# One kernel for two transformer blocks: filter network and short convolution moved inside the first projection, and each norm and operand split moved to the head of the phase that uses it

## The reference

```python
z = rmsnorm(h, mix_norm[j]) @ mix_w_in[j]            # layer 0 of the first block, 3328 columns
y_a = rwkv7_bidir(z[..., :RWKV_COLS], ...)           # 1792 columns
y_b = hyena_bidir(z[..., RWKV_COLS:], ...)           # 1536 columns
h = h + jnp.concatenate([y_a, y_b], axis=-1) @ mix_w_out[j]

def hyena_bidir(z, short_w, short_b, ...):
    u = dwconv_centred(z, short_w, short_b)          # 3 taps along the tokens
    x0, x1, v = u[..., :C], u[..., C:2 * C], u[..., 2 * C:]
    h = hyena_filters(L, ...)                        # 3 sine layers of 64, then 64 -> 2 x 512,
                                                     # times a decay, over the root of its squares' sum
    s = (v * x1)
    y = irfft(rfft(s, 2L) * rfft(kern(h), 2L))[:L] + s * bias
    return y * x0
```

## Time and profile before

| | |
|---|---|
| time, median of 3 runs | 3489.85 us (3485.0 to 3491.21) |
| time of the profiled execution | 3489.5 us |
| its span | 3487.7 us |
| PE busy | 3120.9 us (89%) |
| DVE, ACT, POOL busy | 1628.6, 1314.7, 89.5 us |
| mean granted TensorE clock | 0.925 of full speed |

### The profile page before, as it was taken

How to read it: one execution, slowest core, us unless ns; L and a number is a source line. 1 busy time by engine, 2 the same in 40 slices (tenths; PEclk the granted TensorE clock), 3 DMA queues, 4 the chain that set the end, 5 groups by cost and what they waited for, 6 DMA issues and landing times. The chain is left out here.

```text
span 3487.7 us, 47358 instructions
## 1 busy us (share of the span) xinstructions
PE 3120.9 (89%) x19958; PEld 2433.7 (70%) x19958; DVE 1628.6 (47%) x2294; ACT 1314.7 (38%) x2020; POOL 89.5 (3%) x190
## 2 busy tenths in 40 slices
PE   7948688779999889889999878889999898889999
PEld 5824477767777667667777666567888775568887
DVE  2152555545445346745454336654333348543333
ACT  3210434324333333544333333654424235545151
POOL 0000000001000000000000010000000010100000
PEclk9959777789999999999999989999999899989999
DMA  3110100026444222225444222002323130013222
GB/s 126 63 40 24 41 3 2 3 74 190 162 146 141 89 85 85 76 83 178 164 142 149 76 70 81 1 12 74 100 94 101 52 123 3 1 61 97 97 97 85
DMA packets 223521, 286.67 MB, mean 82 GB/s; under 512 B 7555, under 2 KB 163459, under 8 KB 217172
## 3 DMA queue, kind: packets, MB, share of 16 engines
q1 hardware_dynamic: 214580, 229.73, 20.8%
q0 software_dynamic: 7680, 51.91, 4.3%
q10 hardware_dynamic: 1056, 2.10, 0.2%
HBM read 281.62 MB, written 2.10 MB: 81 GB/s over the span
## 5 line engine op out<-in xcount | busy, mean ns | idle before, releaser
L231 DVE TENSOR_TENSOR weights_low_all<-weights,weights_high_all 128x2048 fp32r<-128x2048 f32 x196 | 449.9, 2295 | 672.1 <-ACT weights_high_all L225 668.4
L225 ACT CAST weights_high_all<-weights 128x2048 fp32r<-128x2048 f32 x196 | 373.5, 1906 | 646.6 <-PE ps L239 636.3
L237 PE MATMUL ps<-ffn_h_high,weights_high_all 128*128 128x512 f32 x704 | 277.8, 395 | 0.9 <-DVE weights_low_all L231 0.9
L239 PE MATMUL ps<-ffn_h_high,weights_low_all 128*128 128x512 f32 x704 | 274.4, 390 | 0.0
L238 PE MATMUL ps<-ffn_h_low,weights_high_all 128*128 128x512 f32 x704 | 274.4, 390 | 0.0
L237 PE MATMUL ps<-mlp_h_high,weights_high_all 128*128 128x512 f32 x512 | 201.0, 393 | 3.1 <-DVE weights_low_all L231 1.8
L239 PE MATMUL ps<-mlp_h_high,weights_low_all 128*128 128x512 f32 x512 | 199.5, 390 | 0.0
L238 PE MATMUL ps<-mlp_h_low,weights_high_all 128*128 128x512 f32 x512 | 199.5, 390 | 0.0
L237 PE MATMUL ps<-weights_high_all,mlp_hid_high 128*128 128x512 f32 x512 | 199.2, 389 | 0.0
L238 PE MATMUL ps<-weights_low_all,mlp_hid_high 128*128 128x512 f32 x512 | 199.2, 389 | 0.0
L239 PE MATMUL ps<-weights_high_all,mlp_hid_low 128*128 128x512 f32 x512 | 199.2, 389 | 0.0
(11 more groups left out here) (548 smaller groups left out, 6373.2 us busy)
## 6 DMA issues: line engine op xcount, KB each, us to landing
mod_w<-in_w_mod POOLq DMA_DIRECT2D x48, 1024.0 KB, 5.2
weights<-in_ffn_w_up SPq DMA_DIRECT2D x88, 512.0 KB, 5.0
weights<-in_w_mlp_in SPq DMA_DIRECT2D x32, 1024.0 KB, 5.5
weights<-in_w_mlp_out SPq DMA_DIRECT2D x32, 1024.0 KB, 5.0
weights<-in_ffn_w_down SPq DMA_DIRECT2D x24, 768.0 KB, 4.4
weights<-in_mix_w_in SPq DMA_DIRECT2D x13, 1024.0 KB, 5.1
weights<-in_na_w_qkv SPq DMA_DIRECT2D x12, 1024.0 KB, 5.2
weights<-in_w_in SPq DMA_DIRECT2D x12, 1024.0 KB, 5.8
```

Of the source, the lines that this page charges most:

```text
L225: nc.scalar.copy(st.high[s][:], st.raw[s][:]).then_inc(st.high_done, 1)
L231: nc.vector.tensor_tensor(st.low[s][:], st.raw[s][:], st.high[s][:], ALU.subtract).then_inc(st.split_done, 1)
L237: nc.tensor.matmul(out, lh, rh, start=start, stop=False)
L239: return nc.tensor.matmul(out, ll, rh, start=False, stop=stop)
```

## The change

What it does, in five parts. First, `MixIn` (on the `Up` class of the feed-forward layers) projects all 13 groups in one phase, unrolled, with the norm at its head; between groups PE does one piece of the filter network, the transposes or the column sums; the first six groups' sums go from PSUM straight through the three taps, and the filter's squares, sums and differences are on POOL. Second, the transform has tables and scratch of its own for the way back, and goes back by frequency tile outermost. Third, `add_product_phase` splits its operand itself and takes tile by tile in its first group; the reload of x is issued by ACT. Fourth, `ple_phase` and `project_heads_phase` begin with `Norm`, whose last four tiles are transposed between the products of the first four. Fifth, the loads of the first two `mix_w_out` groups are no longer held back.

```diff
 def add_product_phase(...):
-                        for t in range(TT):
-                            if q == 0:
-                                pe.wait_ge(added, half * TT + (t + 1))
+                        if half == 0 and q == 0:
                             for k in range(n):
...
+                                pe.wait_ge(tile_low, k + 1)
+                                for t in range(TT):
+                                    mm = product(half, q, t, k, a, False)
...
             @block.scalar
...
+                for k in range(KT):
+                    nc.scalar.copy(split[0][:, k, :], src[:, k, :]).then_inc(tile_high, 1)
                 for g in range(2 * NQ):
...
+                    if x_from is not None and g == 0:
+                        act.wait_ge(tile_low, KT)
+                        act.dma_start(cx.x[:], x_from.rearrange("(t p) c -> p t c", p=P)).then_inc(x_back, 16)
...
+class MixIn(Up):
...
+    FILTER_IN, FILTER_OUT, SQUARES, TURNS = (0, 2, 4), (6, 7), (8, 10), {8: (0, 1, 2), 9: (3,)}
...
+    def pool(self, pool, d, turned):
...
+        for t in range(TT):
+            a, b = (self.taken[:, 2 * (t % 2) + q, :] for q in range(2))
+            pool.wait_ge(self.decayed, 2 * t + 2)
+            if t >= 2:
+                pool.wait_ge(self.sq_sum, t - 1)
+            for q, side in enumerate((a, b)):
+                nc.gpsimd.tensor_tensor(self.square(t, q), side, side, ALU.mult).then_inc(self.squared, 1)
...
+            nc.gpsimd.tensor_tensor(y.h_sum[:, t, :], a, b, ALU.add).then_inc(self.joined, 1)
+            nc.gpsimd.tensor_tensor(y.h_dif[:, t, :], a, b, ALU.subtract).then_inc(self.joined, 1)
...
+    def tensor(self, pe, norm):
+        self.behind(pe, norm)
+        self.beside_tensor(pe, 0)
+        for g in range(1, self.n):
+            self.group(pe, g, lambda j: self.free(pe, g - 2, j) if g >= 2 else None)
+            self.beside_tensor(pe, g)
...
+    def vector(self, dve):
...
+            if g - 1 in self.FILTER_OUT:
...
+                        dve.wait_ge(self.out_sum, n + 1)
+                        if t >= 2:
+                            dve.wait_ge(self.joined, 2 * (t - 1))
+                        nc.vector.tensor_tensor(self.taken[:, 2 * (t % 2) + q, :], ps[:, 4 + n % 4, :], self.decay[:, t, :],
+                                                ALU.mult).then_inc(self.decayed, 1)
...
 def hyena_phase(...):
-                    pe.wait_ge(joined, 2 * TT)
-                    pe.wait_ge(inverse, 32)
...
+                for f in range(TT):
+                    pe.wait_ge(joined, 2 * (f + 1))
+                    for k in range(TT):
                         for q in range(2):
...
 def project_heads_phase(...):
+                norm.begin(pe)
+                G.wait(pe, 0)
+                for k in range(4):
+                    norm.ready(pe, k)
+                    for t in range(TT):
+                        mm = latent(0, t, k) if n_latent else value(0, 0, t, k)
+                    norm.turn(pe, k + 4)
+                mm.then_inc(st.used_up, 1)
+                norm.ready(pe, KT - 1)
...
 def ple_phase(...):
+                            for k in range(4):
+                                norm.ready(pe, k)
...
+                                norm.turn(pe, k + 4)
+                            mm.then_inc(st.used_up, 1)
+                            norm.ready(pe, KT - 1)
+                            turn_p()
```

More of the change, by code:

```diff
@@ L561, in wait_channel_sum @@
         eng.wait_ge(G.st.used_up, g + (G.g0 + 1))
[L564 to L588, removed]
-                    for j in range(2):
-                        wait_channel_sum(act, G, g, j, summed)
-                        nc.scalar.copy(z[:, bass.ds(g * 2 + j, 1), :],
-                                       cx.ps[:, 2 * par + j:2 * par + j + 1, :]).then_inc(copied, 1)
-                each_group(act, G, "high", group)
-            @block.vector
-            def _(dve):
-                each_group(dve, G, "low", lambda g, par: None)
 def token_groups(w, splits):
@@ L1130, in _, with ple_phase @@
                 down.vector(dve)
-def ple_phase(nc, cx, tag, split, p_in):
+def ple_phase(nc, cx, tag, norm, split, p_in):
     st = cx.stream
@@ L1195, in _ @@
             def _(act):
-                for k in range(2):
-                    act.wait_ge(turned, k + 1)
-                    nc.scalar.copy(pT[0][:, k, :], cx.ps[:, 4 + k, :]).then_inc(pT_high, 1)
+                norm.scalar(act)
                 def group(g, par):
@@ new lines, in mix_in_phase, with _ @@
+def mix_in_phase(nc, cx, norm, mix, d):
+    st = cx.stream
+    with nc.Block() as block:
+        @block.sync
+        def _(sp):
+            st.load(sp, st.used + 2)
+        @block.gpsimd
+        def _(pool):
+            mix.pool(pool, d, norm.turned)
+        @block.tensor
+        def _(pe):
+            mix.tensor(pe, norm)
+        @block.scalar
+        def _(act):
+            norm.scalar(act)
+            mix.scalar(act)
+        @block.vector
+        def _(dve):
+            norm.vector(dve)
+            mix.vector(dve)
@@ L1282, in hyena_phase @@
+def hyena_phase(nc, cx, d, y):
     ps = cx.ps
@@ L3335, in ple @@
                 h = parts(hx, f"ple_h{l}")
-                norm_phase(nc, cx, f"pn{l}", gain(f"ple_norm{l}"), split=h)
-                ple_phase(nc, cx, f"ple{l}", h, d["p"][l, 0])
+                xn = hx.enter_context(nc.sbuf_tensor(f"ple_xn{l}", [P, TT, D], F32))
+                norm = Norm(nc, cx, hx, f"pn{l}", gain(f"ple_norm{l}"), h, [xn[:, t, :] for t in range(TT)])
+                ple_phase(nc, cx, f"ple{l}", norm, h, d["p"][l, 0])
         if first <= 0 < last:
```

552 lines of the change are left out of this document (292 added, 260 removed).

## The result

The changed kernel takes 3376.29 us (median of 4 runs, 3375.04 to 3377.17) against 3489.7 before: the ratio is 0.9677, 95% interval 0.966 to 0.9694, so 113 us or 3.2% faster. The forecast was 3366, with 3350 to 3392 around it. The profiled execution took 3376.68 us with a span of 3374.8; its mean granted clock is 0.945 (before 0.925), and PE is busy 92% of the span.

What follows compares the result with a forecast made beforehand. PE was busy 89% of the span, so time was to be had only where it idled or ran slowly; 82.5 + 4.2 + 19.5 − 3.2 + 11.2 + 9.2 = 123.4 off 3489.5 gave 3366.1 us, range 3350 to 3392.

Steps and rivals of the forecast that it cites:

- The mixer: First mixer, from first product to hyena's last DVE operation: 279.1 us against 361.66, a gain of 82.5 us.
- To the transform: First mixer, between projection and transform: copy out of PSUM, square root with its table load, reciprocal and barrier, 2.8 us.
- The work between groups: First mixer: filter network's products 9.4, column sums 6.9 and transposes 1.8 us at full clock between projection groups, together 18.1.
- Thirteen groups: First mixer: the projection's 13 groups of products take 144.0 us; the 16 transposes among them are a separate 1.8.
- Output projections: At no and twice ao, PE starts 5.0 us earlier plus a clock credit, 19.5 us together; mo gains 4.2.
- The 1.5 for the clock: At no and both ao: first group 1.5 us faster each, as PE idles 2 us instead of 7.
- mo's wait for x: In mo, group 1 waits for the reloaded x and a remainder behind it; between 0 and 1.4 us lost.
- Norms at the head: Norms moved into nn, pn and an, with PE idle about 5.1 us before group 1: −3.2, 11.2 and 9.2 us.
- two credits of 8 us at the lower end: Range's lower end, 3350: 8 us if short stalls keep the clock, another 8 if transposes fall where PE waits anyway.
- Rival A: First mixer's projection: PE waits for POOL's chain or DVE's list, up to three stalls, 3384 to 3390 us; chance 0.13.
- B: Rival: the mixer gains as forecast but the other nine sites give nothing, 3407 us; chance 0.07.
- C: Rival: frequent short stalls hold PE at the lower clock for the whole first projection, costing 125 us, 3491; chance 0.03.

Runs made afterwards that it cites:

- e2: Changed kernel with the 32 column sums spread, one behind each three products of groups 9 and 11, instead of two pieces of sixteen; 3372.4 us (0.9667).
- f1: Changed kernel with part four undone, the five norms of ple and the head projections again in phases of their own; 3389.2 us (0.9722).
- f2: Changed kernel with part three undone, operands of mo, no and both ao split in their own phase, SP reloading x; 3401.2 us (0.9749).
- g1: The changed kernel itself, unedited, measured and profiled a second time; 3381.0 us (0.9698).
- g3: Changed kernel with each of POOL's squares, sums and differences done three times; 3389.0 us (0.9719).
- g4: Changed kernel with each of POOL's operations done five times; 3423.2 us (0.9815).

## Why the prediction was right, and where it was off

- **The mixer.** "To the transform" and what follows took 87.6 us as forecast (87.8), and the first product came 0.6 us early. The work between groups took 19.4 us for 18.1: the layers and outputs 10.25 for 9.4, the sums 7.5 for 6.9, the transposes 1.7. The term that was mis-sized is "Thirteen groups", 144.0, with 1.8 for the transposes among them: together they took 152.1 us, 6.3 more. The sum held that work between groups runs at full clock in the company of products; most of it did, but the products behind the two pieces of sums did not. e2 shows 4.8 us of the 6.3. By the starts in the timeline the rest is some 0.4 us more at the lower rate at the head and 0.1 at each of about 14 changes between the kinds of products; no run shows it by itself. No run undoes the mixer's part of the change either: its 75.8 us are read from the traces, and agree with what f1 and f2 leave of the 113 (75 to 85). Nor is there a run for the earlier loads of `mix_w_out` alone.
- **Output projections.** The 5.0 us at each were there (4.85, from 7.0 to 2.1 us of idle time). The 1.5 for the clock was right at one of the three sites in the first profile and at none in g1: the prediction took 2 us of idling as too short for the clock to fall, and it fell 24 times of 30. That the table has 15.6 for the 13.0 at both "ao" is the 2.6 us of the second attention, which no term held. mo's wait for x was 1.11 us, within the 0 to 1.4 given.
- **Norms at the head.** The stall was seen in size and cause: 4.98 at nn for "about 5.1", and the loss at nn 4.0 for 3.2. In ple the term was mis-sized. Group 1 began 22.6 us behind the first transpose and not 21.3, as the four times twelve products and four transposes took 14.2 us for 12.7 (the clock was 0.69 in their first 4 us). The transposes of p fill only 1.1 of the 4.9 us of idle time, and group 1 took 1.8 us longer than before, with the clock at 0.57 in its first 4 us, where 0.8 had been set aside. So 5.6 came out, 2.8 at each, for 11.2.
- **The range's ends, and luck.** Neither of the two credits of 8 us at the lower end came. The recurrence gave 5.0 us by chance and the second attention 2.6 that no term held; without them 3376 would have been 3384, still in the range. So part of the closeness is luck. g1 took back most of the 5.0; there the changed kernel is at 3381, 15 us over the forecast.
- **Rival A** had the mechanism, a chain of POOL that is not done in time, and the slack that the forecast gave it came out in g3. The place was a little off: PE stood at the transposes, released by DVE, and not at the column sums, released by POOL; the latter came only in g4, at the second sums. At the real 1.03 to 1.28 us per operation POOL was done with the first two tiles at 127.2 us, and DVE needs them by 138.2 (2.5 us ahead of the transposes at 140.8): 11 us to spare, though one square did meet DVE's remainder. **B** and **C** are out: f1 and f2 show 8 to 13 and 20 to 25 us from the other sites, and the clock in the projection was 0.97.

## What to carry to other kernels

When a norm or split is moved into the phase that uses it, look at what covers the last tile, and at the order of the two splits behind it: here moving one weight split ahead of the last tiles gave 18 us over five sites, more than moving all five norms had. Price every new idle time of PE with the clock behind it. Filling it with products that nobody reads held the clock at one site of three for certain and gained 1 us there, so measure the stretch around it and not the clock alone. And when two versions differ by a few us, compare stretches between like events, as a stage that neither touches can move by as much: here one moved by 7.7 us.

## What was not expected of the hardware

- At 11 of 12 pieces of 16 one-column fp32 products (3.5 to 4.1 us) the granted clock fell to its lower level with PE busy 100% of the time. In the changed kernel's trace it was back 5.1 and 4.3 us into the full products. One such product behind every three full ones left it at 1.00.
- After the same 2.1 to 2.2 us of idle time the clock fell 24 times of 30 in ten traces. With 8 products in that time it stayed at 1.00 six times of six, though at four of these it may have stayed anyway.
- An operation of POOL and one of DVE on SBUF alone can wait for each other (an addition of 1.04 us took up to 3.16, a DVE step of 0.42 us 1.15).
